# A two-stack transformer kernel on one Trainium2 core: GpSimd in place of VectorE makes the rest halves of layer two's first input weight chunk

## What is computed

```
for l in range(DEPTH):                       # DEPTH = 2
    hx = rms_norm(x, norm1_g[l]) * (1.0 + sc1) + sh1      # 256 latent tokens
    hc = rms_norm(xc, norm1_g[l]) * (1.0 + csc1) + csh1   # 256 context tokens
    y_lat, y_ctx = token_mixers(hx, hc, w_in[l], ...)     # begins with hx @ w_in, hc @ w_in
    x = x + g1 * y_lat
    x = x + g2 * expert_choice_ffn(rms_norm(x, norm2_g[l]) * (1.0 + sc2) + sh2, ...)
    ...                                      # the same for xc in the first layer
```

## Time and profile before

| | us |
|---|---|
| median of 3 runs | 2441.27 |
| lowest and highest | 2440.73 and 2444.0 |
| the profiled execution's own time | 2439.7 |
| its span, first to last instruction | 2437.9 |
| busy: PE, DVE, ACT, POOL | 2227.9, 1114.8, 841.6, 47.4 |
| mean granted share of TensorE's clock | 0.991 |

### The profile page before, as it was taken

One profiled execution on the slowest core, in us unless ns is written; L12 is line 12 of the kernel. 1 busy time (PEld: TensorE's weight loads), 2 busy tenths in 40 slices (PEclk: granted clock), 3 DMA queues, 4 the chain that ended last, 5 costly groups with the idle time before them and its releaser, 6 DMA issues.

```text
span 2437.9 us, 28750 instructions
## 1 busy us (share of the span) xinstructions
PE 2227.9 (91%) x12182; PEld 1478.7 (61%) x12182; DVE 1114.8 (46%) x1640; ACT 841.6 (35%) x1206; POOL 47.4 (2%) x78
## 2 busy tenths in 40 slices
PE   6999999888888999898787879999999999999997
PEld 3865673324232586722131216889998888888887
DVE  4535541112010575501010106868877677757755
ACT  4435421001000455210000005544655465546544
POOL 0022000000000011000000000000000000000000
PEclk9999999999999999999999999999999999999999
DMA  8375369999999641399999997446264454455442
GB/s 328 121 306 211 135 258 398 428 428 427 429 427 428 267 174 47 139 411 428 427 428 429 427 427 300 194 163 233 90 240 164 169 218 179 150 205 194 165 164 87
DMA packets 65055, 660.65 MB, mean 271 GB/s; under 512 B 7264, under 2 KB 9312, under 8 KB 20128
## 3 DMA queue, kind: packets, MB, share of 16 engines
q1 hardware_dynamic: 64928, 658.82, 66.3%
HBM read 657.75 MB, written 1.05 MB: 270 GB/s over the span
## 4 chain that ended last, share of the span: by engine, by line
PE 69%; DMA 23%; DVE 4%; ACT 2%; issue 1%; SPq 0%; DVEq 0%; POOL 0%; ACTq 0%; POOLq 0%
PE ps L774 20%; PE ps L775 10%; PE ps L1187 8%; DMA ring<-in_exp_up 7%; DMA ring_top<-in_exp_up 6%; PE ps L744 5%; PE ps L745 5%; PE ps L746 5%; PE ps L1210 4%; DMA ring_top<-in_exp_gate 3%; DMA ring_top<-in_exp_down 2%; DMA ring<-in_exp_gate 2%; PE ps L1161 1%; PE ps L797 1%; PE ps L925 1%
## 5 line engine op out<-in xcount | busy, mean ns | idle before, releaser
L1187 PE MATMUL ps<-ring,arena 128*32 128x512 f32 (+1 forms) x1184 | 267.0, 598 | 51.7 <-DMA ring<-in_exp_up 26.0
L774 PE MATMUL ps<-h_buf_r,ring_r 128*128 128x512 f32 x800 | 280.2, 396 | 1.6 <-DVE h_buf_r L625 1.5
L2337 DVE TENSOR_TENSOR h_buf<-h_buf,ps 128x512 f32<-128x512 f32 (+1 forms) x32 | 21.9, 683 | 501.8 <-PE ps L1187 501.8
L1187 PE MATMUL ps<-ring_top,arena 128*64 128x512 f32 (+1 forms) x864 | 194.5, 595 | 44.2 <-DMA ring_top<-in_exp_up 22.7
L775 PE MATMUL ps<-h_buf_r,ring_r 128*128 128x256 f32 x800 | 222.4, 278 | 0.0
L1187 PEld LDWEIGHTS ps<-ring,arena 128*32 128x32 f32 (+1 forms) x1184 | 73.5, 123 | 241.3 <-issue 148.6
L774 PE MATMUL ps<-h_buf_r,ring_top_r 128*128 128x512 f32 x608 | 214.3, 397 | 2.9 <-DVE h_buf_r L625 2.9
L404 DVE TENSOR_TENSOR ring_r<-ring,ring_r 128x2048 fp32r<-128x2048 f32 (+4 forms) x84 | 172.7, 2094 | 60.7 <-ACT ring_r L396 60.6
L774 PEld LDWEIGHTS ps<-h_buf_r,ring_r 128*128 128x128 f32 x800 | 150.1, 188 | 37.6 <-issue 1.9
L775 PE MATMUL ps<-h_buf_r,ring_top_r 128*128 128x256 f32 x608 | 170.0, 280 | 0.0
L1187 PEld LDWEIGHTS ps<-ring_top,arena 128*64 128x64 f32 (+1 forms) x864 | 53.7, 124 | 182.6 <-issue 106.0
(11 more groups left out here) (348 smaller groups left out, 4240.6 us busy)
## 6 DMA issues: line engine op xcount, KB each, us to landing
ring<-in_exp_gate SPq DMA_DIRECT2D x39, 2048.0 KB, 29.0
ring<-in_exp_down SPq DMA_DIRECT2D x34, 2048.0 KB, 29.9
ring<-in_exp_up SPq DMA_DIRECT2D x34, 2048.0 KB, 30.2
ring_top<-in_exp_up SPq DMA_DIRECT2D x28, 2048.0 KB, 30.5
ring_top<-in_exp_down SPq DMA_DIRECT2D x26, 2048.0 KB, 28.5
ring_top<-in_exp_gate SPq DMA_DIRECT2D x25, 2048.0 KB, 30.5
ring<-in_ffn_w SPq DMA_DIRECT2D x50, 1024.0 KB, 6.7
ring_top<-in_ffn_w SPq DMA_DIRECT2D x38, 1024.0 KB, 6.7
```

The lines of the kernel that those rows point to most:

```text
L774: release(pe.matmul(ps[:, bank, :], w[0][:, lo:lo + P], both, start=start, stop=False, skip_group_check=True))
L1187: mm = pe.matmul(ps[half * m:half * m + m, which, :], xe[:, k, :], slot(c)[:, at:at + 512], start=k == 0, stop=k == KT - 1)
```

## The change

The two rest halves of layer two's chunk 0 are taken out of VectorE's program and put ahead of everything that GpSimd does in layer two. Since chunk 1's rests count on the same semaphore as chunk 0's, VectorE now waits for both of GpSimd's before it makes them.

```diff
         @block.gpsimd
         def _(pool):
             for l in range(LAYERS):
+                if l:
+                    halve_rest(pool, chunk_at["w_in", l])
                 if l == 0:
...
                 if k == 0 and s == 1 and i:
                     rest(j - 1)
+                    dve.wait_ge(sem("chunk_halved"), halved_before[chunk_at["w_in", 1] + 1])
                     halve_rest(dve, chunk_at["w_in", 1] + 1)
                     dve.wait_ge(sem("norm_std"), i + 1)
                     link(dve.reciprocal(rs[:, at], rs[:, at]))
-                if k == 3 and s == 0 and i:
-                    halve_rest(dve, chunk_at["w_in", 1], 1)
                 dve.scalar_tensor_tensor(in_exact[:, k, at], x_res[:, k, at], gain[:, k, s:s + 1], rs[:, at],
                                          ALU.mult, ALU.mult).then_inc(sem("norm_scaled"), 1)
...
                 experts(l)
-                if l == 0:
-                    halve_rest(dve, chunk_at["w_in", 1], 0)
```

## The result

| | before | changed |
|---|---|---|
| median of 20 runs each, us | 2443.45 | 2450.5 |
| lowest and highest | 2439.21, 2450.16 | 2438.7, 2456.28 |
| profiled execution, its span | 2439.7, 2437.9 | 2451.95, 2450.2 |

The ratio of the runs is 1.0023, 95% interval 1.0012 to 1.0034: the change costs 2.9 to 8.3 us, most likely 5.6. The prediction said 4.4 us, 2445.7 for the time, and 2440.0 to 2448.5 for the range; the median lies above it.

The account below looks back on a forecast made before the run. TensorE, busy 2227.9 of 2437.9 us, was taken as the bound, started at the layer border by VectorE's scalings. Exclusion 4.2 less stop 1.1 plus clock 1.3 made +4.4 on 2441.3: 2445.7 us, range 2440.0 to 2448.5.

Parts of the forecast that it names:

- The first L404 off VectorE: Layer border: VectorE would otherwise wait for the root, so removing its first half-making instruction gives nothing.
- The stop before tile 2: Layer two's projection: TensorE's stop until VectorE's rest of tile 2 goes whole, 1.1 us gained.
- GpSimd's time: Each half's subtraction on GpSimd: 4.7 us taken, from the masks' ratio 2.06 times 2.28 us; ends 2.28 and 9.3.
- The exclusion: GpSimd's second half and VectorE's two-operand scalings shut each other out at the layer border; tile 0 comes 4.2 us late.
- The rival without standing: Path divided or VectorE first, so VectorE runs through at the border: 1.1 us gained, 2440.2 us; chance 0.13.
- The clock: After TensorE's 4 us idle at the border, 1.2 GHz once for 3.4 us, partly within the idle time: 1.3 us lost.
- more of the clock: Rival: low level twice as long, or costing all of it and again: +6.1 us, 2447.4; chance 0.15.
- my case: Main forecast: VectorE shut out and the clock falling once, +4.4 us, own range 2444.2 to 2447.2; chance 0.50.
- It lasts to the end: Behind the layer border nothing gives the delay back or adds to it.
- The added wait: VectorE's semaphore wait ahead of chunk 1's rests has passed by the time VectorE gets there: no cost.
- On the median: The 4.4 us sum is added to the median 2441.27, giving 2445.7 us, +0.18%.
- the highest likely rival: Low clock lasting twice as long or costing all of it and again: 2447.4 us; chance 0.15.

Follow-up runs that it names:

- e1: Against the changed kernel: GpSimd makes the first half alone, VectorE the second before tile 3 as before the change; 2441.26 us, ratio 1.0005.
- e3: Against the changed kernel: 22 matmuls on zeros in place of 4 ahead of layer two's projection; 2446.52 us, ratio 1.0016.
- e4: Against the changed kernel: ScalarE makes both leads early, after layer one, so GpSimd's second half runs before the scalings; 2443.51 us, ratio 1.0007.
- e7: Against the changed kernel: both leads early, GpSimd makes the first half, VectorE the second straight after the residual's additions; 2442.17 us, ratio 1.0004.
- e2: Against the changed kernel: VectorE makes the first half after the additions, GpSimd the second alone; 2450.38 us, ratio 1.0039.
- e8: The changed kernel run once more, nothing altered, timed against the kernel before; 2450.01 us, ratio 1.0024.
- e10: Repeat of the kernel with only the second half on GpSimd and the first on VectorE, timed against the kernel before; 2446.08 us, ratio 1.002.
- e9: The kernel before timed against itself, with a second profile; 2442.01 us, ratio 1.0001.

## Why the prediction was wrong in its number and mostly right in its mechanism

- **The first L404 off VectorE: nothing.** Right, and by e1 the first half on GpSimd is free: 14.79 and 88.48 against 14.79 and 88.47. The sixteen additions, with one operand in the accumulators, kept the 6.92 us that they take before.
- **The stop before tile 2: 1.1 us gained.** Right: 1.13 at tile 2, 1.26 at the turn (e3), 1.23 and 1.25 as the whole effect in e4 and e7.
- **GpSimd's time: 4.7 us, between 2.28 and 9.3.** 4.56 and 4.50. The ratio from the masks was good to 4%. (By the 4497 ns that the Trainium skill gives, page "GPSIMD Engine Reference", section "Performance versus the Vector engine", the trace agrees to 3 ns in the second half.)
- **The exclusion: first rest 4.2 us late.** Right: 4.28, by the way described first, GpSimd ahead by 0.02 us and VectorE shut out at tile 0's scaling; only in e2 does VectorE go first. That the size fits to 0.1 us is in part luck: GpSimd's time was put 0.2 us too long and the overlap at its end 0.2 us too long (0.38 for 0.19), and the two cancel. Exclusion less stop was to be 3.1 us, and e3 measures 3.02. The rival without standing is out. (The Trainium skill, page "SBUF — State Buffer", section "Who interferes with whom", says that whoever has the path keeps it for the whole instruction: the traces agree, with 4.29 us in one direction, and in the other, in e2, with 0.29 us of the 0.42 that tile 0's scaling still had to run when GpSimd began.)
- **The clock: low level once, 1.3 us.** This term was mis-sized: 2.4 us. The step that failed was "the fall may begin within it, where it costs nothing", with a low level of 3.4 us. The fall did begin within the idle time, 1.87 us before the first matmul, but the level stayed low for 6.8 us and not 3.4, so 4.9 us of it fell on work. The three stretches of the earlier trace rows had shown 3.4 us twice, but the clock of the same trace was also low for 6.8 us on end, from 272.5 and from 337.3 on, and I didn't weigh these. The rival with "more of the clock" (6.1 us in all) named this; the truth, 5.4, lies between it and my case. Where the level lasts 3.4 us, in e2, it costs 1.6. Why it lasted 6.8 us here stays open.
- **It lasts to the end.** Right for the border: the 5.39 us at the turn are there at chunk 1 (32.41 - 27.02), and the runs give 5.6 and 5.9. Chunk 1 began at 846.2, which looks like the lower edge of the 846.2 to 847.5 that I named, but this is luck: the changed kernel's profile is 2.26 us ahead of before's at the scatter. On the clock of before it is 848.5, 1.0 us above the upper edge, by the same missing clock term.
- **The added wait: nothing.** Right, released by ScalarE's lead.
- **On the median.** This step failed. I added the sum to a median of three runs, 2441.27, and gave the median itself no width; over 20 runs beside the changed kernel it is 2443.45. Of the 4.8 us between 2445.7 and 2450.5 these are 2.2 and the clock is 1.0. For the last 1.6 no run shows a cause; the scatter of medians is large enough for them (the difference of the medians is 7.05 where the ratio gives 5.6). With 5.4 on 2441.27 the forecast would have been 2446.7, inside the range and still 3.8 low; so the clock term alone does not put the time out of the range, the base with its missing width does. The range ended 1.1 us above the highest likely rival; it should have had on top of each case the 2.5 us by which this kernel's medians move (2441.27, 2443.45, and beside the experiments 2440.92, 2443.2 and 2441.99; the three groups of experiments ran on three different chips, so part of this movement may be the chip's).

## What to carry to other kernels

Work given to an idle engine is not free when the two share a path: price it by what the critical engine runs during it, and place it where that engine has instructions with an operand in the accumulators or none at all (e1, e4). If it can't be moved, cut it: eight pieces cost 0.8 us where one piece cost 5.4. Where a stall of a few us is put in front of TensorE, fill it with matmuls on zeros (e3); the low clock behind it was nearly half of the loss. And give the base its own width before adding a small sum to it.

## What the runs showed of the hardware that I had not expected

- A blocked instruction of VectorE shows the wait as its own duration (4.77, 2.14 and 2.82 us for instructions of 0.48, 0.48 and 0.17): it is in the busy sum, and the view of waits names no releaser.
- The length of the low clock at the border was the same in both executions of one kernel (6.8 us in the changed one and e8, 3.4 in e2 and e10) and differs between kernels whose idle times are alike (4.1 and 3.9 us). But two executions of a kernel are few, and elsewhere it does differ between them: near 340 us the kernel before had 6.8 us of low clock in its first profile and 3.4 in e9, in the same stretch of the code. So the 2.4 us are what this low level cost in two executions, not a fixed price of the change. What sets the length is open. TensorE by stretch, the first profile and then e9 (length, busy and count, clock, DMA):

```profile
337.30:340.70 3.40, 3.40 (x18) 0.50 0.98 419
340.70:344.10 3.40, 3.40 (x18) 0.50 1.04 443
```

```profile
337.80:341.20 3.40, 3.40 (x19) 0.53 0.99 424
341.20:344.60 3.40, 3.40 (x32) 0.97 1.02 436
```

- The steps of 231.6 and 236.0 ns at a granted clock of 1.00 in one and the same code. It is not only the chip: e1 and e2 ran on one, and from 2150 to 2230 us the two largest groups of 128x512 matmuls have a mean of 399 ns in e1 and 394 in e2. What sets the step was not tried.
- No kernel was tried in which GpSimd only writes, so whether that shuts VectorE out is left open.
